# Prompt mixer of a two-layer decoder step: a tile's search bits dealt out as 2, 3, 3, 4, 4, 6, 6, 3 over the eight head slots instead of four in each

## Chip, cores, metric

One core of one Trainium2 chip. The metric is the device time of one execution in microseconds, the median of the runs.

## What is computed

One inference step of a two-layer trunk for a prompt of 1024 tokens and for 64 new tokens of eight cached sequences. Each layer projects the normalised input with one matrix, runs three mixers on parts of the result (a gated linear recurrence, sparse attention, gated linear attention), projects back, and adds an MLP. The part that matters here is the sparse attention of the prompt: for each query the indexer scores all earlier keys, and only the 256 highest take part.

```python
def one_block(args):                      # a block of 128 queries
    q_b, qi_b, wi_b, start = args
    qpos = start + jnp.arange(qb)
    score = index_scores(qi_b, wi_b, ki)
    score = jnp.where(kpos[None, None, :] <= qpos[None, :, None], score, -jnp.inf)
    _, top_i = lax.top_k(score, topk)     # topk = 256
    valid = top_i <= qpos[None, :, None]
    return sparse_attend(q_b, take(k, top_i), take(v, top_i), valid)
```

Attention has eight heads of width 64 over four key heads. A query with at most 256 earlier keys needs no selection, so tiles 0 and 1 (of 128 queries) take all keys.

## The kernel before

The program is written by hand for the five engines: each has one stream of instructions, and they meet through semaphores. A layer has a mixer phase for the prompt, one for the samples' attention, one that projects out, and the MLP. The mixer phase runs over stages `s` = 0 to 10. Stage `s` works on four tiles at once: it finishes the inputs and the two linear mixers of tile `s` (tile 8 is the 64 sample rows), projects tile `s + 1`, searches the threshold of tile `s - 1` (`selects`, tiles 2 to 7, so stages 3 to 8), and does the attention of tile `s - 2` (`attends`). I name a stage by the tile it searches.

A stage is dealt out over the eight heads of the attention, in slots `h` = 0 to 7 and a tail (`h` = 8).

- **DVE** (the loop over `s` and `h` at L1730 and on) begins a slot with `head_max(A_, h)`: it adds the mask to the head's logits out of PSUM, stores the sum and takes its maximum (L1721), and scales it (L1727). The two buffers of `lg` alternate, so head `h` waits for the values of head `h - 2` (L1717 and L1718). In slot 0 the squares of the next heads follow (`head_squares`, L1508 and L1510), then the bits, then the normalised and rotated heads (`heads`, L1515 to L1536). Slot 1 has the convolution (L1549, L1552) and `norm_x` (L1503), slot 2 `gelu_inner` before and `one_minus_a2` (L1571 to L1576) behind the bits, slot 3 `gate_sums` and `recurrence` (L1583 to L1619), slot 4 `gla_operands` (L1626 to L1629), slots 4 and 5 `index_scores` of the next tile to be searched (L1646 to L1652), slot 6 `gla_mask` (L1665), slot 7 `gla_out` (L1672 to L1686). After the slots come the reciprocal of the sums (L1781), the mask from the threshold (L1464 to L1474) and `gla_gate` (L1703 to L1710).
- **The search** (`top_bits`, L1449) finds the 256th highest score of each row bit by bit from the sign down, 31 bits after the sign: the candidate is compared with the scores of a row and the hits are counted (L1454), the count is compared with 256 (L1456), and the candidate corrected (L1458). The three depend on each other, with a drain of DVE after each. The width of a row is 128 x (tile + 1).
- **ACT** takes, in slot `h`, `exp` of head `h` first (L903), then what it copies out of PSUM for the projections, gates and decays, and then the transposed probabilities of head `h - 1` (`probs_out`, L709).
- **TensorE** in slot 1 turns the heads that DVE has made (L1109 to L1117, waits for L1536), in slot 2 the next tile's input (L1080) and the gates (L1132), in slots 3 to 7 one group of projection matmuls each (L1092 or L1096), then in every slot the probabilities of head `h - 1` (L1186), the logits of head `h + 1` (L1178), and the values of head `h - 1` (L1194). In slots 4 and 5 it also makes the dot products for the indexer (L1140), in slot 7 the outputs of the gated linear attention (L1158 to L1167; L1161 and L1172 for the samples), in stage 8 the samples' indexer (L1213 to L1238).
- **POOL** makes inverse roots: of the squares of the heads (L574 and L576) between L1510 and L1515, and it stores results to HBM (L569) in between.

How many bits a slot gets is the tuple `BITS`; the loop takes them from bit 30 downwards:

```python
                        if T_ is not None:
                            top_bits(sc, P, jk, left, left - BITS[h] + 1)
                            left -= BITS[h]
```

The samples' own search has a tuple of its own, `SBITS`, and isn't touched.

Of the kernel before, what the change touches and what calls it, by code (L numbers as in the profile page):

```python
# [41 lines left out]

W_COLS = {"G0": [(C_Q, 512)], "G1": [(C_K, 512)], "C0": [(0, 512)], "G2": [(C_QI, 324), (C_CA, 16)], "C1": [(C_CQ, 256)], "G3": [(C_CV, 512)]}

BITS = (4, 4, 4, 4, 4, 4, 4, 3)
OUT_ORDER = (0, NT) + tuple(range(1, NT))
SBITS = (2, 2, 2, 2, 2, 2, 2, 2)

# [143 lines left out]
def program(nc, D, O, const_at, all_cols):  # L192
# [17 lines left out]
    with ctx, nc.allow_non_contiguous_dma(reason="short vectors and states, element by element"):  # L210
# [1215 lines left out]
        def _(v):  # L1426
# [22 lines left out]
            def top_bits(sc, R, junk, high, low):  # L1449

                for k in range(high, low - 1, -1):
                    ts(junk, sc, cf[:R].bitcast(F32), None, ALU.is_ge, ALU.add, accum_out=cnt[:R])  # L1454
                    D_()
                    ts(ge[:R], cnt[:R], TOPK - 0.5, float(1 << k), ALU.is_lt, ALU.mult)  # L1456
                    D_()
                    stt(cf[:R], ge[:R], (1 << k) >> 1, cf[:R], ALU.bitwise_xor, ALU.bitwise_xor)  # L1458
                    D_()
# [18 lines left out]
            for l in range(DEPTH):  # L1478
# [251 lines left out]
                for s in range(NST):  # L1730
# [4 lines left out]
                    for h in range(8):  # L1735
# [13 lines left out]
# [3 lines that stand above are left out]
                        if s == TILES:  # L1752
# [164 lines left out]
```

## Time and profile before

| | us |
|---|---|
| median of 3 runs | 4069.47 (4065.07 to 4069.73) |
| span of the profiled execution | 4072.7 |
| PE busy in it | 3569.3 (88%) |
| DVE busy | 2124.8 (52%) |
| ACT busy | 1018.2 (25%) |
| POOL busy | 474.9 (12%) |
| the search's counts, L1454, 434 instructions | 500.0 |

The profiled execution spans 4072.7 us, 3.2 us more than the median of the runs. The page gives busy times over the whole program; the two layers' MLPs, where TensorE hardly pauses, fill about half of it, and the stages with a search about a third (twice 645 us). Times below are microseconds from the first instruction. PE is TensorE's matmuls, PEclk is the share of its full clock that was granted (0.5 is 1.2 GHz, 1.0 is 2.4 GHz). In brackets behind a row of the timeline stands how long the engine was idle before it and whose work ended that.

### The profile page before, as it was taken

How to read it: one execution, taken by the hardware profiler on the slowest of the kernel's cores; microseconds unless marked ns; L12 is line 12 of the kernel's file. 1: busy time of each engine (PE TensorE's matmuls, PEld its weight loads, DVE VectorE, ACT ScalarE, POOL GpSimd, SP SyncE). 2: the span in 40 equal slices, each digit the busy share in tenths (PEclk: the TensorE clock that was granted, in tenths of full speed). 3: DMA queues.
4: the chain of work that ended last, by engine and by line, in shares of the span. 5: the costliest groups of instructions: out<-in, count | busy, mean ns of one | idle time of the engine just before them, and what ended most of it. 6: DMA issues, size and time to landing. Idle time of an engine off the chain costs nothing.

```text
span 4072.7 us, 52249 instructions
## 1 busy us (share of the span) xinstructions
PE 3569.3 (88%) x17850; PEld 2698.7 (66%) x17850; DVE 2124.8 (52%) x4881; ACT 1018.2 (25%) x2269; POOL 474.9 (12%) x637
## 2 busy tenths in 40 slices
PE   5778778888799999999987787787787999999999
PEld 3545555556447999999855554555464489999997
DVE  1347778877523444434323577887773334343344
ACT  2232333233401111111123233333234011111110
POOL 0100000221301000000001000002122000000000
PEclk9888888775999999999998888876768999999999
DMA  4000000237621111111410000002465201111111
GB/s 137 15 21 14 14 11 9 46 56 140 208 80 52 42 42 42 54 51 42 140 46 22 14 14 14 11 14 60 41 173 183 88 32 57 48 42 42 42 42 55
DMA packets 189759, 229.61 MB, mean 56 GB/s; under 512 B 72723, under 2 KB 150613, under 8 KB 189493
## 3 DMA queue, kind: packets, MB, share of 16 engines
q1 hardware_dynamic: 161796, 165.17, 15.1%
q0 software_dynamic: 20416, 50.27, 3.9%
q10 hardware_dynamic: 7280, 10.83, 0.8%
q8 instruction: 142, 2.33, 0.2%
q14 instruction: 125, 1.02, 0.1%
HBM read 203.22 MB, written 22.98 MB: 56 GB/s over the span
## 4 chain that ended last, share of the span: by engine, by line
PE 74%; DVE 10%; issue 5%; ACT 5%; DVEq 2%; SPq 1%; DMA 1%; POOLq 1%; POOL 1%; ACTq 0%
PE bank L1389 13%; PE bank L1390 13%; PE bank L1391 13%; PE bank L1096 10%; PE bank L1382 6%; PE bank L1092 5%; PE bank L1194 4%; DVE arena L1454 2%; ACT arena L709 2%; PE bank L1178 2%; DVE arena L1721 1%; PE bank L1186 1%; PE bank L1307 1%; PE bank L1140 1%; SPq L464 1%
## 5 line engine op out<-in xcount | busy, mean ns | idle before, releaser
L1861 DVE TENSOR_TENSOR x_rows<-x_rows,bank 128x512 f32<-128x512 f32 (+1 forms) x576 | 396.1, 688 | 632.1 <-PE bank L1391 632.1
L1096 PE MATMUL bank<-arena 128*128 128x512 f32 (+5 forms) x1440 | 526.5, 521 | 3.0 <-ACT arena L737 1.5
L1454 DVE TENSOR_SCALAR_CACHE_REDUCE arena<-arena,vectors 128x384 bf16<-128x384 f32 (+7 forms) x434 | 500.0, 1152 | 47.5 <-POOLq L406 15.3
L709 ACT ACTIVATE arena<-bank 128x512 f32<-128x512 f32 (+11 forms) x848 | 325.1, 440 | 772.3 <-PE bank L1096 334.0
L1389 PE MATMUL bank<-xT_hi,w_up_hi 128*128 128x364 f32 (+1 forms) x1536 | 506.0, 329 | 5.3 <-DVE vectors L1842 5.3
L1391 PE MATMUL bank<-xT_hi,w_up_lo 128*128 128x364 f32 (+1 forms) x1536 | 506.0, 329 | 0.0
L1390 PE MATMUL bank<-xT_lo,w_up_hi 128*128 128x364 f32 (+1 forms) x1536 | 505.9, 329 | 0.0
L1389 PE MATMUL bank<-w_down_hi,hidden_hi 128*128 128x512 f32 x1152 | 449.5, 390 | 7.5 <-issue 7.5
L1390 PE MATMUL bank<-w_down_lo,hidden_hi 128*128 128x512 f32 x1152 | 449.6, 390 | 0.0
L1391 PE MATMUL bank<-w_down_hi,hidden_lo 128*128 128x512 f32 x1152 | 449.6, 390 | 0.0
L1096 PEld LDWEIGHTS bank<-arena 128*128 128x128 f32 (+1 forms) x1440 | 254.5, 194 | 254.8 <-issue 226.4
L1194 PEld LDWEIGHTS bank<-arena 128*128 128x128 f32 x1152 | 192.5, 255 | 173.4 <-ACT arena L709 138.7
L1194 PE MATMUL bank<-arena 128*128 128x64 f32 x1152 | 212.7, 348 | 100.7 <-ACT arena L709 100.4
L1389 PEld LDWEIGHTS bank<-xT_hi,w_up_hi 128*128 128x128 f32 x1536 | 289.8, 189 | 6.9 <-DVE vectors L1842 5.8
L1390 PEld LDWEIGHTS bank<-xT_lo,w_up_hi 128*128 128x128 f32 x1536 | 289.8, 189 | 1.1
L1391 PEld LDWEIGHTS bank<-xT_hi,w_up_lo 128*128 128x128 f32 x1536 | 289.8, 189 | 0.0
L688 POOL TENSOR_TENSOR hidden_raw<-hidden_raw 128x1088 f32<-128x1088 f32 x64 | 128.0, 2000 | 1335.7 <-ACT hidden_raw L1041 1335.7
L1389 PEld LDWEIGHTS bank<-w_down_hi,hidden_hi 128*128 128x128 f32 x1152 | 217.1, 188 | 52.4 <-issue 8.3
L709 ACT ACTIVATE hidden_hi<-hidden_raw 128x1088 fp32r<-128x1088 f32 x64 | 67.9, 1105 | 722.9 <-PE bank L1391 720.7
L1391 PEld LDWEIGHTS bank<-w_down_hi,hidden_lo 128*128 128x128 f32 x1152 | 217.1, 188 | 45.3
L1390 PEld LDWEIGHTS bank<-w_down_lo,hidden_hi 128*128 128x128 f32 x1152 | 216.9, 188 | 44.0
L1382 PE MATMUL bank<-out_projection 128*128 128x512 f32 x512 | 226.8, 601 | 3.7 <-ACTq L406 3.3
(251 smaller groups left out, 4369.4 us busy)
## 6 DMA issues: line engine op xcount, KB each, us to landing
w_up_landing<-in_w_up SPq DMA_DIRECT2D x32, 1024.0 KB, 7.3
w_down_landing<-in_w_down SPq DMA_DIRECT2D x32, 1024.0 KB, 4.9
arena<-in_cache_k SPq DMA_DIRECT2D x160, 128.0 KB, 2.7
arena<-in_cache_v SPq DMA_DIRECT2D x160, 128.0 KB, 2.6
arena<-in_cache_v POOLq DMA_DIRECT2D x96, 128.0 KB, 3.1
arena<-in_cache_k POOLq DMA_DIRECT2D x96, 128.0 KB, 2.9
arena<-in_w_in ACTq DMA_DIRECT2D x4, 2048.0 KB, 16.1
out_projection<-in_w_out SPq DMA_DIRECT2D x16, 512.0 KB, 9.7
```

The source lines that it names most:

```text
L688: pool.tensor_tensor(hraw[:, i, :], hraw[:, i, :], hraw[:, i, :], ALU.mult).then_inc(s_hsq, 1)
L709: return act.activation(dst, src, ACT.Copy, scale=scale)
L1092: ins = mm(b[:, m * R:(m + 1) * R], w_in[:, c, c0:c0 + P], xnT[:, c, 0:R], start=c == 0, stop=c == 7)
L1096: ins = mm(b[:R, o:o + w], xnT[:, c, 0:R], w_in[:, c, c0:c0 + w], start=c == 0, stop=c == 7)
L1178: mm(b[:, 0:w], QTs[t % 3][64 * j:64 * j + 64, 2 * p + g, :], KT[64 * j:64 * j + 64, p, c0:c0 + w], start=True, stop=True).then_inc(s_full ...
L1194: ins = mm(bank[7][:, 64 * h:64 * h + 64], PT[:, 0, q, :], V[:, q, 64 * (h // 2):64 * (h // 2) + 64], start=q == 0, stop=q == t)
L1382: ins = mm(b[:R, :], yTl[:, t % 2, c, :] if t < NT else yTs[:, c, :], wout[:, c, 512 * n:512 * n + 512], start=c == 0, stop=c == 7)
L1389: mm(out, a[0], b[0], start=first, stop=False)
L1390: mm(out, a[0], b[1], start=False, stop=False)
L1391: return mm(out, a[1], b[0], start=False, stop=last)
L1454: ts(junk, sc, cf[:R].bitcast(F32), None, ALU.is_ge, ALU.add, accum_out=cnt[:R])
L1861: tt(x, x, b[P - R:P, :], ALU.add).then_inc(s_took, 1)
```

## The change

One line: of the 31 bits a tile's search takes after the sign, slots 0 to 7 get 2, 3, 3, 4, 4, 6, 6 and 3 instead of 4, 4, 4, 4, 4, 4, 4 and 3. Both sum to 31.

```diff
-BITS = (4, 4, 4, 4, 4, 4, 4, 3)
+BITS = (2, 3, 3, 4, 4, 6, 6, 3)
```

## Rows read from the trace of the kernel before

**Rows 1.** The page's part 4, the chain that ended last, by engine.

```profile
PE 74%; DVE 10%; issue 5%; ACT 5%; DVEq 2%; SPq 1%; DMA 1%; POOLq 1%; POOL 1%; ACTq 0%
```

**Rows 2.** Stretches: sums over the six search stages, layer 0, then layer 1.

```profile
sum 644.89, PE 508.67 PEld 331.87 DVE 495.88 ACT 206.56 POOL 83.05; mean PE 84.78 PEld 55.31 DVE 82.65 ACT 34.43 POOL 13.84
sum 644.61, PE 509.87 PEld 329.90 DVE 495.87 ACT 206.39 POOL 82.84; mean PE 84.98 PEld 54.98 DVE 82.64 ACT 34.40 POOL 13.81
```

**Rows 3.** Stretches: slot 0 of tile 6's stage; busy by engine, granted clock, DMA.

```profile
660.64:676.49 15.85, 2.44 (x11) 1.21 (x11) 14.05 (x39) 3.36 (x8) 3.78 (x5) 0.66 0.02 8
```

**Rows 4.** Timeline, tile 6, slot 2 to head 3: start, length, engine, line.

```profile
690.66 0.94 ACT L903 ACTIVATE arena<-arena,vectors 128x768 f32<-128x768 f32 x1 [8.83 <-DVE vectors L1727]
698.09 2.82 PE L1194 MATMUL bank<-arena 128*128 128x64 f32 x12 [1.08 <-ACT arena L709]
701.05 0.69 DVE L1721 CUSTOM_DVE_ANT_0 arena<-bank,arena 128x512 f32<-128x512 f32 x1 [1.10 <-PE bank L1194]
```

**Rows 5.** Waits, layer 0's search stages: who for whom, total, times, longest.

```profile
PE bank L1109 <- DVE arena L1536: 72.8, 6, 13.4
DVE arena L1646 <- ACT arena L871: 11.6, 9, 1.9
DVE arena L1721 <- PE bank L1194: 10.6, 10, 2.6
```

**Rows 6.** Timeline, tile 6, slots 5 to 7 of layer 0.

```profile
738.56 0.49 DVE L1646 TENSOR_SCALAR arena<-arena 128x512 f32<-128x512 f32 x1 [1.32 <-ACT arena L871]
753.43 0.94 ACT L903 ACTIVATE arena<-arena,vectors 128x768 f32<-128x768 f32 x1 [6.64 <-DVE vectors L1727]
755.49 1.55 PE L1194 MATMUL bank<-arena 128*128 128x64 f32 x12 [2.25 <-ACT arena L709]
759.71 0.42 DVE L1672 COPY arena<-bank 128x256 f32<-128x256 f32 x1 [1.36 <-PE bank L1162]
```

**Rows 7.** Timeline, tile 6, slot 0: squares, the first two bits, heads.

```profile
664.81 0.95 DVE L1510 TENSOR_REDUCE vectors<-arena 128x12 f32<-128x768 f32 x1
665.68 1.14 DVE L1454 TENSOR_SCALAR_CACHE_REDUCE arena<-arena,vectors 128x896 bf16<-128x896 f32 x1
667.39 1.15 DVE L1454 TENSOR_SCALAR_CACHE_REDUCE arena<-arena,vectors 128x896 bf16<-128x896 f32 x1
...
672.52 0.96 DVE L1515 TENSOR_TENSOR arena<-arena,vectors 128x768 f32<-128x768 f32 x1
```

**Rows 8.** Groups by form: the counts, widest and narrowest tile, busy and mean ns.

```profile
L1454 DVE TENSOR_SCALAR_CACHE_REDUCE arena<-arena,vectors 128x1024 bf16<-128x1024 f32 x62 | 79.2, 1277 | 4.4
...
L1454 DVE TENSOR_SCALAR_CACHE_REDUCE arena<-arena,vectors 128x384 bf16<-128x384 f32 x62 | 37.8, 610 | 4.8 <-issue 0.4
```

**Rows 9.** Timeline, slot 0 of tiles 2, 6 and 7: POOL's power, DVE around it.

```profile
277.19 0.96 DVE L1515 TENSOR_TENSOR arena<-arena,vectors 128x768 f32<-128x768 f32 x1 [1.54 <-POOL vectors L576]
666.37 2.30 POOL L576 TENSOR_TENSOR vectors<-vectors 128x12 f32<-128x12 f32 x1 [0.31 <-issue]
779.73 0.94 DVE L1510 TENSOR_REDUCE vectors<-arena 64x12 f32<-64x768 f32 x1
783.20 2.30 POOL L576 TENSOR_TENSOR vectors<-vectors 64x12 f32<-64x12 f32 x1 [0.73 <-issue]
```

**Rows 10.** Timeline, tile 7, slot 7 of layer 0: maximum and exp of head 7.

```profile
867.99 0.15 DVE L1727 TENSOR_SCALAR vectors<-vectors 128x1 f32<-128x1 f32 x1
870.51 1.03 ACT L903 ACTIVATE arena<-arena,vectors 128x896 f32<-128x896 f32 x1
```

**Rows 11.** Stretches: slot 7 of tile 6, then tile 7, both layers; PEclk third-last.

```profile
751.86:765.65 13.79, 10.94 (x62) 9.90 (x62) 8.90 (x31) 2.88 (x8) 3.49 (x6) 0.71 0.15 33
2771.92:2787.75 15.83, 13.35 (x65) 12.30 (x65) 8.90 (x31) 2.88 (x8) 3.50 (x6) 0.60 0.15 33
866.48:901.65 35.17, 30.00 (x175) 18.78 (x173) 17.73 (x57) 5.49 (x12) 7.34 (x9) 0.71 0.21 56
2889.40:2921.90 32.50, 27.33 (x175) 16.43 (x173) 17.72 (x56) 5.49 (x12) 7.66 (x9) 0.79 0.22 60
```

## The prediction, made before the changed kernel was run

> **What bounds the kernel now.** I read the page first: the chain that ended last is three quarters TensorE and a tenth DVE [rows 1], so only the stretches in which DVE ends last can pay. The change touches DVE's order in twelve such stretches, six stages in each of the two layers. The stretch table says how long they are: 644.9 us in layer 0 and 644.6 us in layer 1, with DVE busy 495.9 us and TensorE 509 us of each [rows 2]. Neither fills the time, so they wait for each other. Then I followed one stage, that of tile 6, in order of time, and looked in the other stages for where the same joins differ.
>
> A slot, here, runs from one head's maximum on DVE to the next head's. Four joins decide a stage. (1) In slot 0 the head normalisation of the next tile (L1515) stands behind the first search bits, and TensorE can turn the heads only when it is through: TensorE is all but idle until then, 2.4 us busy of 15.9 [rows 3]. (2) In slot 2 ACT starts on exp as head 2's maximum is in, does the gates, copies the probabilities of head 1, TensorE multiplies them, and only then may head 3's maximum run: DVE stands idle 1.10 us in front of it [rows 4]. (3) In slots 4 and 5 DVE waits for the index scores (L1646), in nine places of layer 0 and 11.6 us in all [rows 5]. (4) In slot 7 the engines are a chain that starts at head 7's maximum: exp of head 7, copies, values of head 6, the GLA output (DVE idle 1.36 us before L1672) and so to the end of the stage [rows 6]. ACT takes the exponential before the copies for head 6, so what delays head 7's maximum delays all of this.
>
> **What the change is.** The bits still sum to 31, so no instruction is added or lost, and every step of the search reads the same scores: each tile's threshold is the same. A bit costs the distance between two counts: 667.39 less 665.68 is 1.71 us at tile 6 [rows 7]. The counts take 610 ns at 384 columns and 1277 ns at 1024 [rows 8]; with the other 0.57 us of a bit (1.71 less the 1.14 of its count) that is 1.18 us for tile 2 and 1.85 for tile 7, evenly spaced between: 1.31, 1.45, 1.58, 1.71 for tiles 3 to 6. After slots 0 to 7 DVE has done 2, 3, 4, 4, 4, 2, 0 and 0 bits less than before. DVE's work in a stage is the same, so a stage changes by its waits alone.
>
> **Slot 0, two bits less.** Four bits lay between L1510 and L1515. They also hid POOL, which makes the inverse roots: at tile 6 its power operation ends 2.9 us after L1510 (666.37 + 2.30 against 664.81 + 0.95) [rows 7, 9], and two bits are 3.4 us, so the heads come 3.4 us earlier. At tile 2 POOL starts late and DVE already waits 1.54 us; there two bits less bring nothing. At tile 7 POOL ends at 785.50, 4.8 us after L1510 (779.73 + 0.94); DVE would be there 3.6 us after it, so of the 3.7 us of two bits some 2.3 remain [rows 9]. In layer 1 POOL is 2 us later at tile 6 (a store before it), which leaves 2.0.
>
> **Slot 1, one bit less.** DVE was the later one at head 2, with 1.1 to 5 us to spare before TensorE, so this bit adds its full price to the lead, except at tile 7, where TensorE comes first into play (1.3 of 1.85). At tile 6 head 2's maximum is 3.4 + 1.7 = 5.1 us earlier.
>
> **Slot 2, one bit less.** Nothing. Head 3 hangs on ACT and TensorE, both released by head 2 [rows 4]; DVE's wait of 1.10 us becomes 2.8. The lead at head 3, and through slots 3 and 4, whose joins all hang on it, is then 1.2, 3.4, 4.1, 4.7 and 5.1 us for tiles 2 to 6 (3.7 at tile 6 of layer 1), and 3.3 for tile 7.
>
> **Slots 5 and 6, two bits more each.** What DVE waited there is room. At tile 6 it is 1.32 us before L1646 in slot 5 [rows 6]. Of the two groups of waits, for index scores and of the maxima for values [rows 5], I took from each stage what lies in slots 5 and 6; the rest lies before head 3 and in slot 4, where it stays. Head 7's maximum at tile 6 is then at -5.1 + 4 x 1.71 - 1.3 = +0.4 us. Tile 2 has room for all it gets (the longest wait of a maximum, 2.6 us, is its head 7 [rows 5]). For the others the same sum, with 1.9, 1.4, 0.8 and 0 us of room for tiles 3, 4, 5 and 7, gives +0.1, +0.3, +0.9 and +4.1 us at head 7; at tile 6 of layer 1 (room 1.0) +2.2, at tile 5 of layer 1 (room 1.2) +0.5.
>
> **Slot 7, as before.** What of that reaches the end depends on what the values of head 6 waited for. At tiles 5 and 6 it was exp of head 7: all of it. At tile 7 ACT was busy with copies, the maximum was done at 868.14 and its exp began at 870.51 [rows 10], so 2.4 of 4.1 us go under. At tiles 2 to 4 the last one was TensorE with the projection before, which has the lead: the end comes 1.2 us earlier for tile 2, 1.9 for tile 3 (from there head 7 is the later one), 2.7 for tile 4 in layer 0 and 1.2 in layer 1. Layer 0: -1.2 -1.9 -2.7 +0.9 +0.4 +1.7 = -2.8. Layer 1: -1.2 -1.9 -1.2 +0.5 +2.2 +1.7 = +0.1. Together -2.7 us. The stages stand end to end, and I found nothing between them that would take up a shift.
>
> **TensorE's clock in slot 7.** There is a second price. TensorE, ahead by its lead, finishes its part of slot 7 sooner and now waits longer for exp of head 7: at tile 6 some 6 us where it waited 2.25 [rows 6]. The trace has the same slot at both levels of the clock. At tile 6 the mean grant was 0.71 in layer 0 and 0.60 in layer 1, and the slot took 13.79 and 15.83 us; at tile 7 0.71 and 35.17 us, against 0.79 and 32.50 [rows 11]. A fall to the lower level (1.2 for 2.4 GHz) right after the wait therefore costs 2.0 and 2.7 us. Bounds: none of the late slots changes its level (0), or all six of tiles 5 to 7 do (about 13). Three of them already ran low in that place (tile 7 in layer 0, tiles 5 and 6 in layer 1); the other three I count as new, as each waits as long as or longer than those: 2 + 2 + 2.7 = 6.7, tile 5 priced like tile 6. The Trainium skill (TensorE: Matmul & The Clock Gate, "HAM oscillation — how this bites in real kernels") says that waits of the array between bursts of matmuls put it back to the half clock, each time anew; by that rule this change, which makes such waits longer, pays at every late slot, and [rows 11] bear it out in size though not in every stage.
>
> **Sum.** -2.7 + 6.7 = +4.0 us. On the profiled execution's 4072.7 us this is 4076.7; the runs' median is 4069.5, 3.2 lower, so 4073.5 us.
>
> **Rivals.** *Opposed terms nearly cancel* (the forecast): the time stays within 8.1 us, which is 0.2% and about what a measurement of this kernel can tell from no change. *The lead is kept:* POOL keeps up, the clock rises sooner because TensorE starts earlier in slot 0, and slots 5 and 6 have more room than I found, since late index scores and values are also waits of TensorE. Then each stage gains what it has at head 3 less a little; the leads of both layers sum to 42 us, and a half of it would be -21: about 4050 us. For it speaks that DVE waits in slots 5 and 6 in the narrow tiles; against it that tiles 5 to 7 have hardly any wait there. *Late slots overfull* (the slower side): one mechanism, head 7's maximum held back by slots 5 and 6, whose place is ACT's exp of head 7 [rows 6]. It decides from the point at which the lead at head 3 is smaller than four bits less the room (about 5.5 us at tiles 5 and 6). If the lead turned out one bit smaller in every stage, because head 2 too waits for TensorE or ACT, the wide tiles 4 to 7 lose 1.45 + 1.58 + 1.71 + 1.85 = 6.6 us in each layer, +13 on top of +4: 4086 us. If slots 0 to 2 gave nothing at all, four bits less room would be lost everywhere, 25 us a layer, 4120; what speaks against that is TensorE's wait for the heads, 72.8 us in six stages, 13.4 the longest [rows 5]: whatever brings the heads forward brings TensorE forward. *Not what it says:* excluded, the sums are equal and the order is a plain loop.
>
> **Chances.** Forecast 0.60 (4062 to 4077), lead kept 0.12, late slots overfull 0.28, most of it between 4078 and 4090. So faster 0.12, same 0.60, slower 0.28. For 8 in 10 the range reaches a little to both: 4060 to 4087.
>
> **What would show it.** In the profile after: at tile 6 heads turned 3.4 us earlier in the stage, at tile 7 a new wait of DVE for POOL before L1515, at tile 2 a longer one; waits before head 3 longer by one bit; no wait left before L1646 of slot 5 in tiles 3 to 7; the stages of tiles 2 to 4 shorter by 1 to 3 us, those of tiles 5 to 7 longer by 0 to 5; and a longer wait of TensorE before the values of head 6 with a lower grant behind it. I am wrong if the stages of tiles 5 to 7 get shorter, or if head 2's maximum doesn't move by slot 0's gain plus a bit.

## The result, and the profile after

The changed kernel takes 4094.64 us (4090.81 to 4097.38), 4068.32 before on the same chip: a ratio of 1.0062 [1.0048 to 1.0077], so 26 us slower. The forecast was 4073.5, the range ended at 4087. Its profiled execution spans 4095.7 us, 23.0 more than that of before.

I looked first where the 23.0 us lie. The stretches view has us, busy time of each engine with the number of instructions, PEclk, DMA share and GB/s; here are the stages of tiles 4 and 5 in layer 0, then the sums over the six search stages of layer 0 and of layer 1:

```profile
447.45:550.46 103.01, 85.23 (x363) 56.79 (x362) 77.77 (x237) 32.18 (x87) 9.05 (x12) 0.80 0.04 14
550.46:662.15 111.69, 91.70 (x405) 63.00 (x404) 86.14 (x262) 34.60 (x95) 9.05 (x12) 0.82 0.03 10
...
sum 655.34, PE 522.39 PEld 342.17 DVE 495.55 ACT 205.75 POOL 87.53; mean PE 87.07 PEld 57.03 DVE 82.59 ACT 34.29 POOL 14.59
...
sum 656.89, PE 520.95 PEld 339.45 DVE 495.30 ACT 205.46 POOL 87.48; mean PE 86.82 PEld 56.57 DVE 82.55 ACT 34.24 POOL 14.58
```

Against [rows 2] that is 10.4 + 12.3 = 22.7 us, so all of it is in the stages that the change touches. DVE's work is the same (495.55 for 495.88 us): only waits changed, as forecast. Stage by stage, in us, the forecast with its clock term:

| tile | layer 0: forecast | measured | layer 1: forecast | measured |
|---|---|---|---|---|
| 2 | -1.2 | -4.0 | -1.2 | -1.5 |
| 3 | -1.9 | -1.5 | -1.9 | -0.9 |
| 4 | -2.7 | **+2.6** | -1.2 | **+5.9** |
| 5 | +2.9 | **+5.2** | +0.5 | **+5.4** |
| 6 | +2.4 | +2.4 | +2.2 | +1.8 |
| 7 | +1.7 | **+5.8** | +4.4 | +1.7 |

The miss is 18.7 us in all. Tiles 4 and 5 miss by 19.6 together; the other eight miss by -2.8 to +4.1 us each and cancel but for 0.9. Next, who waits for whom. The waits of DVE in layer 0's search stages (who for whom: us in total, times, longest), after:

```profile
DVE arena L1672 <- PE bank L1162: 16.8, 6, 7.1
DVE arena L1515 <- POOL vectors L576: 15.4, 5, 5.6
DVE arena L1721 <- PE bank L1194: 12.0, 10, 2.5
...
DVE arena L1646 <- ACT arena L871: 7.6, 5, 2.2
```

and two lines of the same view of before:

```profile
DVE arena L1672 <- PE bank L1162: 21.9, 6, 9.1
DVE arena L1515 <- POOL vectors L576: 1.5, 1, 1.5
```

L1646 went from nine waits to five, which lie in slot 4 (forecast: none left in slot 5; [rows 5]). The new one is POOL: 15.4 us where there were 1.5, and 11.5 in layer 1 where there were 1.5. By tile, in layer 0: 3.87 (tile 2), 0.50, 3.60, 1.91, 0 and 5.56 us; in layer 1: 3.87, 0.50, 2.98, 2.57, 1.56 and 0. The forecast had 3.9 twice at tile 2, 1.2 twice at tile 7 and 1.4 at tile 6 of layer 1, which is 11.6 us. Tiles 4 and 5 weren't in it: 11.1 us.

**Why POOL is late.** The timeline (start, length, engine, line; in brackets the idle time before it and who ended that) from the end of tile 3's stage into slot 0 of tile 4, which begins at 447.45. After:

```profile
441.82 9.31 PE L1096 MATMUL bank<-arena 128*128 128x512 f32 x16
450.96 0.38 PE L1291 MATMUL bank<-cst,arena 128*128 128x128 f32 x2
452.98 0.54 POOL L569 DMA_DIRECT2D y_scratch<-arena  x1 [12.54 <-ACT arena L709]
455.18 0.20 POOL L574 TENSOR_SCALAR vectors<-vectors 128x12 f32<-128x12 f32 x1 [1.65 <-DMA y_scratch<-arena]
455.69 2.30 POOL L576 TENSOR_TENSOR vectors<-vectors 128x12 f32<-128x12 f32 x1 [0.32 <-issue]
458.03 0.96 DVE L1515 TENSOR_TENSOR arena<-arena,vectors 128x768 f32<-128x768 f32 x1 [3.60 <-POOL vectors L576]
```

The same place before, where tile 4 begins at 453.72:

```profile
446.07 7.13 PE L1096 MATMUL bank<-arena 128*128 128x512 f32 x16
453.65 0.44 PE L1291 MATMUL bank<-cst,arena 128*128 128x128 f32 x2 [0.44 <-DVE arena L1710]
455.41 0.54 POOL L569 DMA_DIRECT2D y_scratch<-arena  x1 [8.33 <-ACT arena L709]
458.09 0.20 POOL L574 TENSOR_SCALAR vectors<-vectors 128x12 f32<-128x12 f32 x1 [2.14 <-DVE vectors L1510]
458.61 2.30 POOL L576 TENSOR_TENSOR vectors<-vectors 128x12 f32<-128x12 f32 x1 [0.32 <-issue]
```

Read it from the bottom. POOL has one queue. In it, ahead of the inverse roots for the next heads (L574, L576), stand the store of the previous tile's last part (L569) and a wait for its landing. That part comes from the transposes at the end of the stage (L1291), and these stand on TensorE behind the tail's projection of 16 matmuls (L1096). Before, the projection took 7.13 us and was over when the stage began; the store had landed when DVE's sum of squares (L1510) was in, and the roots hung on DVE. After, the same matmuls take 9.31 us and end 3.7 us into the stage, so the roots hang on the store. The end of the tail came 4.2 us later in the stage: 2.2 are its own slower matmuls, the other 2.0 are that it began 5.6 us before the stage's start and not 7.7. What is left of the bits in slot 0 doesn't cover that.

Why the matmuls are slower is seen one slot earlier. Slot 7 of tiles 3 and 5, before:

```profile
435.62:446.47 10.85, 9.56 (x71) 8.05 (x70) 7.06 (x28) 2.03 (x6) 1.24 (x3) 1.00 0.00 0
...
641.34:651.79 10.45, 8.84 (x71) 7.95 (x70) 8.37 (x31) 2.89 (x8) 1.24 (x3) 1.00 0.00 0
```

and after:

```profile
431.12:440.20 9.08, 6.34 (x37) 5.32 (x35) 7.06 (x27) 1.91 (x6) 1.60 (x3) 0.77 0.00 0
...
639.73:653.30 13.57, 9.48 (x44) 8.64 (x45) 8.37 (x31) 2.67 (x8) 1.84 (x3) 0.62 0.00 0
```

The granted clock falls from 1.00 to 0.77 and 0.62. TensorE's wait in that slot, for ACT's copies behind exp of head 7, rose from 0.65 to 2.10 us at tile 3 and from 0.81 to 5.98 at tile 5. The row of tile 3, before and after:

```profile
440.08 0.88 PE L1194 MATMUL bank<-arena 128*128 128x64 f32 x6 [0.65 <-ACT arena L709]
```

```profile
433.44 0.88 PE L1194 MATMUL bank<-arena 128*128 128x64 f32 x6 [2.10 <-ACT arena L709]
```

The grant was 1.00 through the wait and 0.50 from 436 to 445, over the end of slot 7 and most of the tail. What I had priced as a clock dip inside slot 7 of the wide tiles happens from tile 3 on, and its dearer part is paid a stage later on two other engines.

At tile 7 of layer 0 the late one is the store's landing itself; the store was issued earlier in the stage than before (2.2 us into it for 3.6). Timeline after:

```profile
781.40 0.54 POOL L569 DMA_DIRECT2D y_scratch<-arena  x1 [8.71 <-ACT arena L709]
790.36 0.19 POOL L574 TENSOR_SCALAR vectors<-vectors 64x12 f32<-64x12 f32 x1 [8.42 <-DMA y_scratch<-arena]
791.28 2.30 POOL L576 TENSOR_TENSOR vectors<-vectors 64x12 f32<-64x12 f32 x1 [0.73 <-issue]
```

The same wait was 2.87 us before. The queues carry the samples' small packets there in both kernels (DMA share 0.31 over the stage before, 0.32 after). In the 14 us around the store the two loads of `in_consts` took 8.9 us to land at the median, and 2.8 before, so other transfers were slow at that moment too; why at that moment isn't shown. Where the lead of a stage isn't eaten in this way the forecast's steps are there. Tile 6 of layer 0, slot 0 and head 3:

```profile
662.15:674.55 12.40, 3.37 (x13) 1.56 (x11) 11.11 (x31) 3.30 (x8) 4.57 (x5) 0.74 0.03 11
```

```profile
697.06 0.69 DVE L1721 CUSTOM_DVE_ANT_0 arena<-bank,arena 128x512 f32<-128x512 f32 x1 [2.47 <-PE bank L1194]
```

Slot 0 took 15.85 us [rows 3] and takes 12.40, 3.4 less as forecast. Head 3 comes 5.5 us earlier (forecast 5.1), behind a wait of 2.47 us (forecast 2.8).

### The profile page after: what moved, and what is told of

The parts are those of the page before. It is cut to its first block, busy times and chain, and to the rows that moved or that the text cites. A ratio compares the mean times of both kernels' runs of the same rounds, so it can differ in the third digit from the quotient of the medians.

```text
span 4095.7 us, 52249 instructions
## 1 busy us (share of the span) xinstructions
PE 3598.6 (88%) x17850; PEld 2720.9 (66%) x17850; DVE 2123.6 (52%) x4881; ACT 1016.8 (25%) x2269; POOL 484.4 (12%) x637
## 4 chain that ended last, share of the span: by engine, by line
PE 71%; DVE 11%; issue 5%; ACT 4%; DMA 2%; DVEq 2%; SPq 1%; POOL 1%; POOLq 1%; ACTq 0%
PE bank L1389 13%; PE bank L1390 13%; PE bank L1391 13%; PE bank L1096 11%; PE bank L1382 6%; PE bank L1194 4%; DVE arena L1454 4%; PE bank L1092 3%; PE bank L1178 2%; ACT arena L709 2%; DVE arena L1721 1%; PE bank L1186 1%; PE bank L1307 1%; DMA y_scratch<-arena 1%; DMA arena<-in_cache_k 1%
## 5 line engine op out<-in xcount | busy, mean ns | idle before, releaser
L1096 PE MATMUL bank<-arena 128*128 128x512 f32 (+5 forms) x1440 | 536.1, 528 | 3.0 <-ACT arena L737 1.5
L1454 DVE TENSOR_SCALAR_CACHE_REDUCE arena<-arena,vectors 128x384 bf16<-128x384 f32 (+7 forms) x434 | 499.9, 1152 | 48.6 <-POOLq L406 15.4
L1096 PEld LDWEIGHTS bank<-arena 128*128 128x128 f32 (+1 forms) x1440 | 258.2, 197 | 262.5 <-issue 234.4
L903 ACT ACTIVATE arena<-arena,vectors 128x256 f32<-128x256 f32 (+7 forms) x128 | 99.1, 774 | 528.4 <-DVE vectors L1727 521.6
```

The lines of the kernel that those rows point to most:

```text
L903: act.activation(x, x, ACT.Exp, bias=small[:, 64 + h % 2:65 + h % 2], scale=0.125, accum_out=small[:, 80 + h:81 + h]).then_inc(s_p, 1)
L1096: ins = mm(b[:R, o:o + w], xnT[:, c, 0:R], w_in[:, c, c0:c0 + w], start=c == 0, stop=c == 7)
```

## The experiments

The theory, A: the loss beyond some 4 us is the late inverse roots of POOL, behind the slow tail. The rival, B: the loss is made in the late slots themselves, by head 7's maximum and TensorE's clock, and POOL's wait only shows a delay that is there anyway.

**1. POOL's queue reordered, the deal as changed.**

The lines go up from the end of POOL's loop body (for the tile before, `o`), and the two lines of `rstd`, the inverse root of the next tile's input, go up with them.

```diff
                         inv_root(small[:R, 20:32], small[:R, 32:44], 1.0 / 64).then_inc(s_krs, 1)
+                    if s + 1 < TILES:
+                        rstd(s + 1)
+                    if 1 <= s <= TILES:
+                        o = s - 1
+                        if o < NT:
+                            pool.wait_ge(s_evac, A_AT[l, o, "yc"] + 1)
+                            store(y_part(o, 6, 2), yC[:, o % 2, :, :])
+                        stored(s_yst)
...
-                            pool.wait_ge(s_evac, A_AT[l, t, "yc"] + 1)
-                            store(y_part(t, 6, 2), yC[:, t % 2, :, :])
-                        stored(s_yst)
```

> The changed kernel, with POOL's order changed: the inverse roots of the next heads (and of the next tile's input) come before the store of the previous tile's last output part and the wait for its landing. Theory A (the two bits taken from slot 0 uncovered POOL, which stands behind that store; the store is late because TensorE's tail work of the stage runs at the lower clock): DVE's waits before L1515, 15.4 and 11.5 us in the two layers of the changed kernel, fall under 3 us together, and the time falls by 12 to 22 us, to about 4075 to 4083. Theory B (slots 5 and 6 are overfull; POOL's lateness lies in time that slots 1 and 2 would wait anyway): the waits before L1515 fall, but come back before head 3 and in slot 7, and the time stays within 5 us of 4094.

Measured: 4049.48 us (4067.25 before on that chip), a ratio of 0.9959 [0.9947 to 0.9971], 45 us less than the changed kernel. DVE's waits for POOL in the search stages fall from 15.4 and 11.5 us to 2.3 and 1.1, and the place shown above has become, with the tail as slow as in the changed kernel, 9.29 us (3 lines more stand above, so L1518 is L1515; POOL's rows first, then DVE's):

```profile
440.57 0.20 POOL L574 TENSOR_SCALAR vectors<-vectors 128x12 f32<-128x12 f32 x1 [11.40 <-DVE vectors L1513]
441.00 2.31 POOL L576 TENSOR_TENSOR vectors<-vectors 128x12 f32<-128x12 f32 x1 [0.23 <-issue]
...
445.42 0.63 POOL L569 DMA_DIRECT2D y_scratch<-arena  x1
...
443.33 0.96 DVE L1518 TENSOR_TENSOR arena<-arena,vectors 128x768 f32<-128x768 f32 x1 [0.16 <-POOL vectors L576]
```

B, as put there, falls. A's number fails too: it had 12 to 22 us, and 45 us are more than the change had cost. In the search stages it is 23.9 us (642.1 and 646.2 us now). The other part lies in stages without a search, where no bits cover POOL in either kernel: in tile 1's stage DVE waited 7.04 us for the roots and now waits 2.87, and the stage went from 79.3 to 75.1 us. So the even deal had to be measured in the new order too.

**2. POOL's new order with the even deal.** The edit of 1 on the kernel before.

> The kernel before (four bits in each slot) with POOL's new order: inverse roots first, store of the previous tile's last part after. Theory A (the change costs what it does because it uncovered POOL): with POOL out of the way the new deal of the bits is worth having, so this run lies above the 4049.5 us of the changed kernel in the same order, by 3 to 15 us: 4052 to 4065; most of its own gain comes from stages without a search, where nothing covers POOL. Theory B (late slots overfull): the deal costs its 26 us here too, and this run lies near 4025 to 4035, below 4049.

Measured: 4045.65 us (4067.99), 0.9942 [0.9929 to 0.9956]. Neither expectation: the even deal also gains 22 us, and the changed deal is 3.8 us above it by the medians. By the two ratios it is 7 us, give or take 7, so this pair of times by itself hardly tells the two deals apart. In the search stages of the profiled executions the new order takes 5.7 us from the even deal and 23.9 from the changed one. So of the 22.7 us that the change cost there, **18.2 come through POOL and 4.5 are the deal's own** (one profiled execution each; the ratios of whole runs give 18 for the first part too, give or take 9). The 18.2 hold the waits for POOL that the forecast had counted as well. The pair also shows the deal by itself, in us that a maximum comes later (+) or earlier (-) in its stage of layer 0:

| tile | head 3: forecast | after against before | experiment 1 against 2 | head 7: forecast | after against before | 1 against 2 |
|---|---|---|---|---|---|---|
| 3 | -3.4 | -3.7 | -3.7 | +0.1 | +0.2 | -0.1 |
| 4 | -4.1 | **-0.8** | -4.3 | +0.3 | **+3.6** | 0.0 |
| 5 | -4.7 | **-2.9** | -4.8 | +0.9 | +2.1 | -0.7 |
| 6 | -5.1 | -5.5 | -5.5 | +0.4 | +1.6 | +0.5 |
| 7 | -3.3 | **+0.3** | -4.4 | +4.1 | **+8.5** | +3.8 |

With POOL out of the way the slots of layer 0 behave nearly as worked out up to head 7. In layer 1 head 7 came at +2.2, +0.5, -1.2, +0.7 and +1.9 us for tiles 3 to 7, where the forecast had +0.1, +0.3, +0.5, +2.2 and +4.1.

**3. TensorE kept busy in slot 7.** If the slow tail comes from the wait in slot 7, work put into that wait should undo it, with POOL's order untouched.

```diff
-                def project(t, i):
+                def project(t, i, again=0):
...
-                        for m, c0 in enumerate((0, 128, 256, 384) if key == "C0" else (C_CQ, C_CQ + 128)):
...
+                        for _ in range(1 + again):
+                            for m, c0 in enumerate((0, 128, 256, 384) if key == "C0" else (C_CQ, C_CQ + 128)):
...
-                                project(s + 1, 6)
+                                project(s + 1, 6, 1 if s >= 3 and s < NT else 0)
```

> The changed kernel, with the projection group of slot 7 computed twice into the same bank in the stages of tiles 2 to 6, so that TensorE works through most of its wait for exp of head 7 in the wide stages. The result is the same. If the lower clock after that wait is what makes the tail of the stage late (part of theory A), the grant in slot 7 and the tail rises in tiles 4 to 6, the tail's projection takes 7.1 us instead of 9 or more, the waits before L1515 fall in the stages after it, and the time falls by 3 to 10 us although TensorE does 3.7 us more in each of ten stages. If the clock plays no part, tiles 2 and 3, where TensorE comes last, lose up to 3.7 us each: 4098 to 4105.

Measured: 4093.07 us, 1.0069 [1.0049 to 1.0089]: nothing in total, and so between the two expectations. But the link is there. Slot 7 of tiles 3 and 4, then 6, and the tail of tile 3:

```profile
435.42:446.23 10.81, 9.52 (x70) 8.03 (x70) 7.06 (x27) 2.03 (x6) 1.23 (x2) 1.00 0.01 2
534.29:544.05 9.76, 8.27 (x63) 7.14 (x62) 7.59 (x27) 2.44 (x6) 1.23 (x3) 1.00 0.01 2
...
753.97:773.20 19.23, 18.04 (x80) 16.83 (x80) 8.89 (x30) 3.11 (x8) 3.49 (x6) 0.50 0.14 32
```

```profile
445.84 7.13 PE L1097 MATMUL bank<-arena 128*128 128x512 f32 x16
```

The grant is 1.00 at tiles 3 and 4 in both layers (0.77 and 0.68 in layer 0 of the changed kernel, 0.72 and 0.60 in layer 1). TensorE's wait at tile 3 is 0.65 us as before, the tail starts 7.6 us before the stage again and takes 7.13 us. DVE's wait for POOL at tile 4 falls from 3.60 and 2.98 to 0.24 and 0.23 us, and that stage from 103.0 and 104.6 to 98.6 and 98.5. The Trainium skill (TensorE: Matmul & The Clock Gate, "HAM oscillation — how this bites in real kernels") says that waits between bursts of matmuls put the array back to the half clock; these stretches agree, the grant going from 1.00 to 0.77 with the longer wait and back to 1.00 with the wait filled. Where the extra matmuls themselves run at the lower clock they only cost: slot 7 of tile 6 takes 19.23 us for 14.55. Tiles 2, 3 and 6 get 1.2 to 3.9 us longer each; tile 3's 1.7 and 1.2 us are what the fill costs where it makes tile 4's 4.4 and 6.1 us.

So the fill was tried only in the stages whose next stage waits for POOL (`s in (5, 6)`, tiles 4 and 5):

> The changed kernel (POOL's old order) with slot 7's projection computed twice only in the stages of tiles 4 and 5 (the same result). With it in five stages, tile 4's stages were 4.4 and 6.1 us shorter and tile 5's 1.8 and 3.7, tiles 2, 3 and 6 longer. Clock as a cause: here those gains stand alone, tile 4's tail runs at the full clock and the next stage's wait for POOL goes: 8 to 16 us less than 4094, 4078 to 4086. If the gains were chance between executions: 4090 to 4098.

Measured: 4087.55 us, 1.0041 [1.0026 to 1.0057], 7.1 less than the changed kernel and a little short of the expectation; the two intervals overlap, so this gain isn't clear of noise. The stages of tile 4 are only 1.3 and 1.5 us shorter and its waits stay (2.8 and 3.0 us), since tile 3's slot 7 isn't filled here: the 4.4 and 6.1 us were made by the fill one stage earlier. Behind the filled slot of tile 4 the tail took 7.13 us in layer 0, where tile 5's wait for POOL is gone, but 8.53 in layer 1, where 1.6 us of it stay.

**4. Single moves of bits.** Two bits from slot 0 to slot 5 alone:

```diff
-BITS = (4, 4, 4, 4, 4, 4, 4, 3)
+BITS = (2, 4, 4, 4, 4, 6, 4, 3)
```

> The kernel before with 2, 4, 4, 4, 4, 6, 4, 3: only the part of the change that moves two bits from slot 0 to slot 5. Theory A: slot 0 gains little, as DVE then waits for POOL; slot 5 has one to two us of room; I expect it close to the kernel before, -4 to +6 us. Theory B (late slots overfull, loss grows with the bits moved late): also near 0, since slot 6 keeps four bits; then the loss of the full change comes from slot 6.

Measured: 4069.29 us (4067.25), 1.0008 [0.9998 to 1.0019]: what slot 0 gives, slot 5 takes. Its trace also shows slot 0 with two bits where head 7 is at most 2.0 us late (8.5 in the changed kernel): DVE waits 7.8 and 7.3 us for POOL in the two layers, and at tile 4, behind a tail of 7.13 us, only 0.24 and 0.23. In POOL's new order the same deal gives

> POOL's new order, with 2, 4, 4, 4, 4, 6, 4, 3: only slot 0 gives, only slot 5 takes. Slot 5 has 0.8 to 1.5 us of room, slot 6 stays as it was. Expected: 3 to 12 us less than the changed deal in this order (4049.5), since the bits from slots 1 and 2 bring one bit of lead at the most and cost two in slot 6: 4037 to 4047.

4031.70 us, 0.991 [0.9897 to 0.9924], 14 us below the even deal in that order and better than expected; the new order is worth 38 us with this deal. Then one bit from slot 2 to slot 6:

```diff
-BITS = (4, 4, 4, 4, 4, 4, 4, 3)
+BITS = (4, 4, 3, 4, 4, 4, 5, 3)
```

> The kernel before with 4, 4, 3, 4, 4, 4, 5, 3: one bit moved from slot 2 to slot 6. By my sum the bit from slot 2 brings nothing (head 3 hangs on ACT and TensorE) and slot 6 has room only in tiles 2 and 3, so it costs about a bit in each of tiles 4 to 7: 1.45 + 1.58 + 1.71, and nothing or a part at tile 7 (ACT has 2.4 us to spare there), in each layer: +8 to +13 us. If instead slot 2 does give its bit on, the time stays within 3 us.

Measured: 4075.57 us, 1.0024 [1.0013 to 1.0034], 8.3 us slower. The step "slot 2: nothing" holds: with a bit less there head 3's maximum doesn't move in tiles 2 to 6 (0.7 us earlier in tile 7). At head 7 the bit in slot 6 is paid nearly in full or more, 1.0 to 2.1 us in tiles 3 to 7, but it reaches the end of the stage only at tiles 5 and 6 (2.6 and 4.1 us in layer 0, 3.0 and 0.7 in layer 1).

**5. The freed bits put behind head 7's maximum.** In slot 7 DVE waits for TensorE before the GLA output, 21.9 us in six stages before. A bit in slots 5 and 6 delays head 7's maximum; a bit in slot 7 stands behind it, in that wait.

```diff
-BITS = (2, 3, 3, 4, 4, 6, 6, 3)
+BITS = (2, 4, 4, 4, 4, 4, 4, 5)
```

With POOL's new order:

> POOL's new order, with 2, 4, 4, 4, 4, 4, 4, 5: the two bits of slot 0 go to slot 7, where DVE waits for TensorE before L1672 anyhow. Head 7's maximum is then two bits earlier in every stage instead of up to four bits of late work behind it. If head 7's maximum sets the end of the wide stages (my fourth join), this beats both deals in this order: 4030 to 4045 us. If the bits in slot 7 only stand before L1672 themselves, it is within 5 us of 4049.

Measured: **4013.78 us** (4006.21 to 4018.41; 4067.99 before), 0.9862 [0.9847 to 0.9878]: 54 us below the kernel before and the fastest of all. DVE's waits in layer 0 of experiment 2, then of this one:

```profile
DVE arena L1675 <- PE bank L1165: 22.3, 6, 6.3
DVE arena L1649 <- ACT arena L874: 11.6, 9, 1.9
DVE arena L1724 <- PE bank L1197: 9.1, 10, 2.5
```

```profile
DVE arena L1724 <- PE bank L1197: 12.9, 11, 2.8
DVE arena L1649 <- ACT arena L874: 12.5, 9, 2.3
DVE vectors L1784 <- PE bank L1197: 6.0, 2, 5.7
DVE arena L1675 <- PE bank L1165: 3.9, 2, 2.6
```

The wait before the GLA output (L1675) falls from 22.3 to 3.9 us, and head 7's maximum keeps its lead (4.0 us at tile 6, 4.5 at tile 5). The stages sum to 630.5 and 622.6 us.

The same deal in POOL's old order:

> POOL's old order, with 2, 4, 4, 4, 4, 4, 4, 5: the deal that took 4013.8 us in the new order. Slot 0 gives two bits as in the change, nothing is put into slots 5 and 6. Theory A: POOL's lateness came from two things together, little cover in slot 0 and a late tail after a late head 7. Here the second is gone, so the loss against the new order is what it is for the even deal, 18 to 26 us (the even deal: 4068.0 against 4045.7), and a little more: 4032 to 4046, faster than the kernel before. If two bits in slot 0 were by themselves what uncovered POOL, the loss is 35 us and more: 4050 to 4070.

4052.94 us (4065.22), 0.9963 [0.9952 to 0.9974]. It gains 12 us, but less than theory A said; the time lies in the second range, that of two bits less in slot 0 uncovering POOL by themselves. The waits for POOL are there again in layer 0 (4.6 us in layer 1):

```profile
DVE arena L1515 <- POOL vectors L576: 8.7, 5, 3.9
```

So the new order is worth 22 us with four bits in slot 0, 38 and 39 with two, and 45 with the full change. In the search stages of the traces that is 5.7, 13.1, 16.7 and 23.9 us. Theory A therefore has two parts. As an estimate from these four differences, 7 to 11 of the 18.2 us that the change lost through POOL come with two bits less in slot 0 alone. The other 7 to 11 come only with the rest of the change, by which TensorE is further ahead and head 7 later, with the longer wait and the slow tail behind it. DVE's waits for POOL in the old order, both layers together, say the same: 15.1 and 13.3 us in the two runs with two bits in slot 0, for 11.6 forecast, and 26.9 in the changed kernel.

With four bits in slot 0 and the two bits for slot 7 taken from slot 6 (4, 4, 4, 4, 4, 4, 2, 5), old order:

> POOL's old order, with 4, 4, 4, 4, 4, 4, 2, 5: two bits from slot 6 to slot 7, slot 0 untouched. Head 7's maximum comes two bits earlier in the stages of tiles 3 to 7, the bits after it fill DVE's wait before L1672. Gain where head 7 set the values of head 6 (tiles 5 and 6, up to 2.2 us before TensorE comes last, less what the bits overfill in slot 7): 0 to 2 us a stage, 0 to 8 in all: 4060 to 4068.

4064.90 us, 0.9999 [0.9989 to 1.0008]: slot 7's room alone brings nothing; with slot 0's lead the same two bits there gained 12 us above. Two that put still more there, in POOL's new order, (2, 4, 4, 4, 4, 4, 3, 6) and (2, 4, 4, 4, 4, 3, 3, 7):

> POOL's new order, with 2, 4, 4, 4, 4, 4, 3, 6: one more bit from slot 6 to slot 7 than in the run of 4013.8 us. There DVE reached L1672 with no wait left in tiles 3 to 6 (0.07 us), and 1 to 4 us in tiles 2 and 7. So the sixth bit delays the end in tiles 4 to 6 by what is not given back by an earlier head 7: -4 to +8 us against it, 4010 to 4022.

> POOL's new order, with 2, 4, 4, 4, 4, 3, 3, 7. Slot 7 overfull: two bits more before L1672 in tiles 3 to 6, 2.6 to 3.4 us a stage less what slots 5 and 6 give: 5 to 20 us above 4013.8, 4019 to 4034.

4024.37 us, 0.9894 [0.9877 to 0.991], and 4039.08, 0.994 [0.9926 to 0.9954], both above what I expected and above the five bits: slot 7 is full at five.

## Why the prediction was wrong

The sign came out as forecast, the size didn't: +4.0 us forecast, +23.0 in the profiled execution, +26 by the medians.

- **What bounds it, and DVE's work the same:** right; 22.7 of 23.0 us are in the twelve stages, with equal work.
- **Slot 0, two bits less: the step that failed.** It took the time at which POOL's roots are ready from the trace of before, in every tile, and left out that the change itself makes the store ahead of them later, by TensorE's longer wait for head 7 and the slow tail behind it. It gave some 2.7 us at tile 4 and 3.1 at tile 5 (the leads at head 3 less a bit); the heads came 0.3 us later and 1.3 earlier in layer 0, 0.0 and 0.7 earlier in layer 1. Tile 7 of layer 0 was to give 2.3 and lost 1.7, by the slow landing. Its term for POOL (11.6 us of waits) measured 26.9; in the two runs that only take the two bits from slot 0, it measured 15.1 and 13.3. Where POOL wasn't late, or was late as forecast, the step holds to 0.2 us: 3.44 at tile 6 for 3.4, 2.02 in layer 1 for 2.0, and nothing at tile 2. Tile 7 of layer 1 gave 3.7, since POOL was ready there.
- **Slot 1 at full price, slot 2 at nothing:** right. Head 2 at tile 6 came 5.5 us earlier for 5.1, and one bit moved from slot 2 to 6 cost 8.3 us (experiment 4).
- **Slots 5 and 6:** right in layer 0 where slot 0 was right; head 7 was forecast within 0.4 us at tiles 3, 4, 6 and 7 and within 1.6 at tile 5 (1 against 2 in the table). In layer 1 it was off by up to 2.3 us. Two slips of addition are in that paragraph and the one before: the terms of tile 3 give -0.1 at head 7 and not +0.1, and those of tile 7 a lead of 3.6 and not 3.3. In the changed kernel itself it was 1.2 us later at tile 6 than forecast, 1.2 of which is slot 4 (16.06 us for 14.83), where the index scores were late.
- **TensorE's clock:** the mechanism was right, its place and its price were not. I let it begin at tile 5 and counted the slot alone. It fell at tiles 3 and 4 too, and its main effect there and at tile 5 was the tail projection at 8.4 to 9.5 us for 7.13, ahead of the transposes that POOL's store waits for. Experiment 3 shows that link from slot 7 to tail and to DVE's wait; experiment 1 that the price passes through POOL. At tile 6 TensorE waited 2.37 us before the values of head 6, not some 6, and still the grant fell from 0.71 to 0.58.
- **The sum as a number:** +4.0 forecast, +3.8 between experiments 1 and 2, +4.5 in their stages. That this agrees is in good part luck. The forecast had POOL late by 11.6 us, in experiment 1 it is late by 3.4; and stage by stage the two differ by 0 to 3.7 us (tile 2 of layer 1: -1.2 forecast, -4.9; tile 3: -1.9, +1.3; tile 6: +2.2, +4.5), which cancels in the sum.
- **The rivals:** late slots overfull was the side it came out on, but not the mechanism: POOL ate the lead in slot 0, and so tiles 4 and 7 arrived at slots 5 and 6 without it, with the effect that rival described (a lead smaller than the bits added). The two theories of the experiments meet here, since TensorE's wait for head 7 is what slowed the tail ahead of the store. The lead kept was out of reach in this deal; with POOL and slot 7 put right it is real, since experiment 5 is 1.8 to 5.2 us a stage shorter than experiment 2 in ten of the twelve stages (tiles 2 and 3 of layer 0 are 0.6 and 0.2 longer).

Two stages came out 2.8 and 2.7 us better than forecast, tile 2 in layer 0 and tile 7 in layer 1. The traces show where. Slot 7 of tile 2 took 8.63 us for 12.02, at a grant of 1.00 for 0.88. Tile 7 of layer 1 had POOL ready early, and the clock term of 2.7 us didn't come: its slot 7 took 32.75 us for 32.50, though the grant fell from 0.79 to 0.69. Why, stays open; no run was made for these.

## What to carry to other kernels

Bits, or any filler, ahead of a join cover not only the wait that the trace shows but every queue that was just in time behind it: before thinning them out, write down for each engine released there when it would have been ready *in the changed order*, with a store and its landing counted as part of an in-order queue. A clock dip must be priced by what is queued behind the slower matmuls on other engines too, not only by the slot in which it happens. And a freed piece of work belongs behind the event that releases the other engines (here head 7's maximum), in a wait that is already there.

## What the runs showed of the hardware

- The same 16 matmuls of 512 columns took 7.13 us after a slot granted 1.00 and 9.31 after one granted 0.77, in which TensorE had waited 2.10 us (0.65 before). I had not expected a dip behind so short a wait.
- Matmuls that compute nothing new held the grant at 1.00 in slot 7 of tiles 3 and 4, and tile 4's stage was 4.4 and 6.1 us shorter (experiment 3). At tile 5 the grant stayed low (0.69 and 0.62), and at tile 6 it was 0.50 throughout and the slot 4.7 us longer.
- A store of 128 KB by POOL took 2.20 us from the start of its instruction to the release of the waiting POOL at tile 4, and 8.96 at tile 7 among the samples' packets (3.41 before). The Trainium skill (DMA: Bandwidth & Descriptors, "Anatomy of one DMA — SWDGE (gpsimd) path") gives about 2 us as the fixed part of such a transfer, mostly its completion; tile 4 agrees, tile 7 is over four times that.
- POOL's power took 2.30 us for 128x12 values and the same for 64x12, 1.03 for 128x4, and 0.56 or 0.97 for 128x1. So it goes with the columns and not with the partitions.
